# All 32 of layer 1's late modulation partial sums in layer 0's mixers, none in layer 1's projection

## What is computed

```
cond = jax.nn.silu(c)
for layer in range(DEPTH):
    mod = cond @ ada_w[layer] + ada_b[layer]
    sh1, sc1, g1, sh2, sc2, g2 = [m[:, None, :] for m in jnp.split(mod, 6, axis=-1)]
    h = rms_norm(x, norm_mix[layer]) * (1 + sc1) + sh1
    mix = mix_gla_gdn(h, ...) if layer % 2 == 0 else mix_swa(h, ...)
    x = x + g1 * mix
    h = rms_norm(x, norm_ffn[layer]) * (1 + sc2) + sh2
    x = x + g2 * moe(h, ...)
```

## Time and profile before

| | |
|---|---|
| median of 3 runs | 1645.1 us (1643.97 to 1645.26) |
| the profiled execution | 1644.02 us |
| its span | 1642.1 us |
| PE busy | 1373.0 us (84%) |
| DVE busy | 1102.9 us (67%) |
| ACT busy | 705.5 us (43%) |
| chain that ended last, by engine | PE 73%, DVE 13%, ACT 5%, DMA 5%, issue 3% |

### The profile page before, as it was taken

How to read it: one execution, slowest core, us unless ns; L and a number is a source line. 1 busy time by engine, 2 the same in 40 slices (tenths; PEclk the granted TensorE clock), 3 DMA queues, 4 the chain that set the end, 5 groups by cost and what they waited for, 6 DMA issues and landing times.

```text
span 1642.1 us, 15877 instructions
## 1 busy us (share of the span) xinstructions
PE 1373.0 (84%) x6192; PEld 1049.0 (64%) x6192; DVE 1102.9 (67%) x1258; ACT 705.5 (43%) x865; POOL 363.6 (22%) x135
## 2 busy tenths in 40 slices
PE   5899976759776987999999664976889689999992
PEld 1587765559664465888888542434764568888882
DVE  3757676567554464999899628675415659999994
ACT  1212333232123133777777521123642257777771
POOL 2100000000000000566664411000000015665641
PEclk9879987969888977999999876996979689999997
DMA  9678327120200354999999336253000659999964
GB/s 347 229 260 289 96 81 265 39 77 14 116 1 0 129 228 155 368 384 374 373 376 362 119 110 251 88 190 156 1 0 27 234 213 366 381 373 380 387 239 167
DMA packets 63440, 338.42 MB, mean 206 GB/s; under 512 B 11738, under 2 KB 11818, under 8 KB 49284
## 3 DMA queue, kind: packets, MB, share of 16 engines
q1 hardware_dynamic: 50868, 310.54, 50.8%
q0 software_dynamic: 11680, 23.43, 4.1%
q10 hardware_dynamic: 816, 3.43, 0.6%
HBM read 326.34 MB, written 28.84 MB: 216 GB/s over the span
## 4 chain that ended last, share of the span: by engine, by line
PE 73%; DVE 13%; ACT 5%; DMA 5%; issue 3%; POOL 1%; SPq 0%; DVEq 0%; ACTq 0%; POOLq 0%
PE ps L1333 12%; PE ps L1334 11%; PE ps L1335 11%; PE ps L1203 7%; PE ps L894 6%; PE ps L1225 5%; PE ps L901 2%; ACT work L1478 2%; PE ps L903 2%; PE ps L902 2%; DMA ring<-in_ada_w_dram 2%; DVE early_mod L2022 2%; PE ps L1251 1%; ACT work_r L1478 1%; PE ps L1280 1%
## 5 line engine op out<-in xcount | busy, mean ns | idle before, releaser
L801 POOL TENSOR_TENSOR work<-work,early_mod 128x1024 f32<-128x1024 f32 x33 | 175.7, 5324 | 181.0 <-ACT work L1478 181.0
L1335 PE MATMUL ps<-ring_r,work_r 128*128 128x512 f32 x536 | 214.4, 400 | 0.0
L1478 ACT ACTIVATE work<-ps 128x512 f32<-128x512 f32 (+4 forms) x142 | 90.8, 646 | 286.3 <-PE ps L1335 165.3
L894 PE MATMUL ps<-const,work 128*128 128x128 f32 x792 | 127.7, 306 | 98.9 <-DVE work L1994 29.9
L1333 PE MATMUL ps<-early_mod_r,work_r 128*128 128x512 f32 x468 | 189.4, 405 | 10.8 <-DVE work_r L2600 4.7
L2295 DVE TENSOR_TENSOR ring_r<-ring,early_mod_r 128x2048 fp32r<-128x2048 f32 x76 | 177.9, 2371 | 27.1 <-ACT early_mod_r L1478 26.6
L1334 PE MATMUL ps<-early_mod_r,work_r 128*128 128x512 f32 x468 | 186.6, 399 | 0.0
L894 PEld LDWEIGHTS ps<-const,work 128*128 128x128 f32 x792 | 107.4, 161 | 122.4 <-DVE work L1994 28.7
L1478 ACT ACTIVATE work_r<-ring 128x2048 fp32r<-128x2048 f32 (+2 forms) x87 | 133.2, 1555 | 56.3 <-PE ps L903 56.0
L1478 ACT ACTIVATE early_mod_r<-ring 128x2048 fp32r<-128x2048 f32 x79 | 147.5, 1908 | 0.0
L1333 PE MATMUL ps<-work_r 128*128 128x512 f32 x324 | 132.5, 409 | 7.3 <-DVE work_r L2600 4.9
(11 more groups left out here) (329 smaller groups left out, 2712.1 us busy)
## 6 DMA issues: line engine op xcount, KB each, us to landing
ring<-in_moe_w_up_dram SPq DMA_DIRECT2D x33, 2048.0 KB, 10.3
early_mod<-in_ada_w_dram SPq DMA_DIRECT2D x80, 512.0 KB, 4.5
ring<-in_moe_w_gate_dram SPq DMA_DIRECT2D x19, 2048.0 KB, 10.0
hT<-in_moe_w_down_dram SPq DMA_DIRECT2D x16, 2048.0 KB, 9.9
ring<-in_moe_w_down_dram SPq DMA_DIRECT2D x15, 2048.0 KB, 9.9
work<-in_moe_w_gate_dram SPq DMA_DIRECT2D x14, 2048.0 KB, 10.4
ring<-in_ab_w_in_dram SPq DMA_DIRECT2D x7, 2048.0 KB, 9.8
ring<-in_ada_w_dram SPq DMA_DIRECT2D x4, 2048.0 KB, 23.7
```

What stands on the lines that cost most here:

```text
L801: return nc.gpsimd.tensor_tensor(yb[buf], yb[buf], mod[:, 5 * D:6 * D], ALU.mult)
L894: return nc.tensor.transpose(dst, src, ident[0:k, 0:k])
L1335: return mm(out, a_hi, w_lo, start=False, stop=last_)
L1478: return nc.scalar.activation(out, in_, fn, **kw)
```

## The change

It moves the boundary `SIDE_B` from 8 to 10, so that units 64 to 79 join units 48 to 63 in the mixers, and `project_swa` holds none. The counts in the mixers become 8, 5, 2, 5 and 3 after each of four levels, 32 in all. The four blocks' sums lie in the four row tiles of `x`. With the blocks 8 and 9 gone from layer 1, SP issues no side load there, the wait for all puts ahead of L776 becomes a wait for the end of `project_swa` (`phase_done` 18), and so does POOL's wait ahead of L883. POOL's second clearing of `side_pad` is taken out.

```
-        SIDE_B = 8
+        SIDE_B = len(SIDE)
...
-            for c in ((1, 1, 1, 1, 1) if t + 1 < TT else (1, 0, 0, 0, 0)):
+            for c in (0, ) * 5:
...
             if SIDE_A <= i < SIDE_B:
-                return x.rearrange("p t d -> p (t d)")[:, 1024 * (i % 2):1024 * (i % 2) + 1024]
+                return x[:, i - SIDE_A]
...
-            for u in range(KD * SIDE_B, KD * len(SIDE)):
-                side_load(u)
-            side_put(len(SIDE) - 1)
             load_columns(("swo", 1), a["swa_w_out"][0], range(0, D, 512))
-            sp.wait_ge(side_out, 16 * len(SIDE))
+            sp.wait_ge(phase_done, 3 * 6)
             sp.dma_start(mod[:, 2048:6144], sum_rows[1][:, 2048:6144]).then_inc(sums_in[2], 16)
...
             pool.wait_ge(moe_done, 1)
-            nc.gpsimd.memset(side_pad, 0.0).then_inc(pad_ready, 1)
             norm_shift(1)
-            pool.wait_ge(side_out, 16 * len(SIDE))
+            pool.wait_ge(phase_done, 3 * 6)
             nc.gpsimd.dma_start(gain2, bc(a["norm_ffn"][1])).then_inc(gains_in[1], 16)
...
             def gla_gates():
-                mix_sides(5)
+                mix_sides(8)
                 dve.wait_ge(GATE_ACT.sem, GATE_ACT.at(0, "l"))
...
                 ins.then_inc(GATE_DVE.sem, GATE_DVE.one("zg"))
-                mix_sides(3)
+                mix_sides(5)
...
                         dve.wait_ge(GLA_DVE.sem, GLA_DVE.at(t, f"s{c}"))
-                mix_sides(1)
+                mix_sides(2)
                 dve.wait_ge(GLN_ACT.sem, GLN_ACT.at(0, "ss3"))
...
-                mix_sides(3)
+                mix_sides(5)
                 dve.wait_ge(PRE_ACT.sem, PRE_ACT.at(0, "expa"))
...
                     if l < 5:
-                        mix_sides(1)
+                        mix_sides(3)
```

## The result

| | before | changed |
|---|---|---|
| median | 1644.86 us, 4 runs (1643.97 to 1645.26) | 1662.6 us, 4 runs (1657.41 to 1665.14) |
| ratio | | 1.0104, interval 1.0082 to 1.0126 |
| profiled execution | 1644.02 us, span 1642.1 | 1663.34 us, span 1661.4 |
| granted TensorE clock, mean | 0.892 | 0.886 |

The change costs 17.7 us by the medians and 19.3 by the two profiled executions. The prediction was 1658.8 in a range of 1652 to 1665, so the median lies inside the range, near its upper end.

What follows compares the result with a forecast made beforehand. PE was taken to bound layer 1's projection, side sums and their loads the chain at the mixers' gates. Terms 5.8 + 1.1 + 1.4 + 4.1 + 1.9 = 14.3 us, nothing saved, gave 1658.3, median put at 1658.8, range 1652 to 1665.

Steps and rivals of the forecast that it cites:

- Taken out: Layer 1's projection: removing sixteen DVE units, 20.5 us, and their loads gains 0, at most 0.8 us, since PE bounds it.
- Moved later: Read-backs of both layers' sums, the reload of `x` and the `gain2` load start later but are covered: 0.
- Gates: Ahead of the gate, 5 units become 8; DVE time and loads start the gate 5.8 us later.
- Behind the gate: Between the gate and the next DVE step, 3 units become 5: 1.1 us late, bounds 0 and 3.3.
- Loop: Behind GLA's loop, 1 unit becomes 2; the variance waits for DVE: +1.4 us.
- `gdn_pre`: In `gdn_pre`, 3 units become 5, the last two waiting for loads: +4.1 us, bounds 3.8 and 6.8.
- Inverses: At four levels, 1 unit becomes 3; DVE needs 11.2 us against PE's 10.72: +1.9 us, bounds 1.0 and 3.0.
- The clock: PE's granted clock: level changes may fall a few matmul groups earlier or later; 0, bound 3 us either way.
- a stage beyond 533 us changes by more than 1 us: Sign that would show the forecast wrong: a stage later than 533 us whose length changes by over 1 us.
- The mixers absorb it: Rival: 57 us of idle DVE in the mixers takes the units, time stays 1644 to 1646; chance 0.07.
- The projection pays it back: Rival: units held up PSUM banks in layer 1's projection; removing 22.2 us of them gives 1636; chance 0.04.
- Loads bind harder: Rival: fourth units meet 7.5 us load landings and PE stays at low clock longer: about 1667; chance 0.12.

Runs made afterwards that it cites:

- the gates' half: Changed kernel with eight units left in layer 1's projection: 8, 5, 1, 3 in the mixer groups and 2, 2, 2, 1 a level; 1653.55 us, ratio 1.0048.
- the second trace: The changed kernel run again, unedited, beside the kernel before; 1657.54 us over 6 runs, ratio 1.0087.
- the levels' half: Changed kernel with eight units left in layer 1's projection: 5, 3, 1, 3 as before and 3 a level; 1650.81 us, ratio 1.0044.
- The delay: Kernel before with 15 clearings of `kz` added on DVE ahead of the gate, no side unit or load more; 1664.41 us, ratio 1.011.
- the one with 5, 4, 0 and 3: Kernel before with the output projection's weight chunks behind the side loads, sixteen mixer units at 5, 4, 0, 3 and one a level; 1643.77 us, ratio 0.9986.

## Why the prediction held, and where it did not

**Taken out: 0, and 0 measured.** The kernel without the sixteen units measured it directly, 0.9999.

**Moved later: 0.** SP's read-back was issued at 1134.75, 17.8 us after PE's last matmul of the projection at 1116.9, where "some 17 us later" was the estimate. The fold that needs it ran at 1230.02, 95 us on, and took its usual 3.49 us. The row of SP's queue:

```profile
1134.75 0.34 SPq L773 DMA_DIRECT2D early_mod<-sum_rows  x1
```

**Gates: 5.8 predicted, 6.4 and 6.8 measured**, 5.8 with one unit a level, and 5.2 in the gates' half. The mechanism is the predicted one, load by load; unit 51's load took 8.14 us instead of 7.78, and unit 55's 4.73 instead of 4.5. The pieces of the chain that are loads, here and in the two later groups:

```profile
271.74 8.14 DMA early_mod<-in_ada_w_dram
...
282.60 4.73 DMA early_mod<-in_ada_w_dram
...
294.79 5.45 DMA early_mod<-in_ada_w_dram
...
350.34 5.15 DMA early_mod<-in_ada_w_dram
```

**Behind the gate: 1.1, and 1.1** (1.3 in the second trace). **Loop: 1.4, and 1.4** from the first unit's start to the variance (2.59 us against 1.21), while the loop itself was 0.3 shorter. **`gdn_pre`: 4.1, and 4.1** (5.1 in the second trace, where the last load took 6.10 us instead of 5.15). **Inverses: 1.9, and 1.7**, with DVE's period of 11.2 us a level measured as 11.16. Together 14.3 predicted, 14.25 measured to `ku_b`, 16.3 in the second trace. That 14.3 met 14.25 so closely is in part luck: the gate cost 0.6 more, the loop and the inverses less, and the second trace is 2.0 away. What the terms are made of is shown: the gates' half gave the gates' two terms without the others, the levels' half that of the inverses alone, and the kernel with 8, 5, 2 and 5 but one unit a level the groups without the inverses, those of the loop and `gdn_pre` among them. These two were not tried one by one. The delay showed that lateness at the gate reaches the end.

Two sums of the prediction are off by little. It put the median 1.1 us above the profiled execution and yet arrived at 1658.8, where 1658.3 + 1.1 is 1659.4, and its inverses (423.2 against 421.2) give 2.0 and not 1.9.

**The clock: 0 with a bound of 3, and that is the mis-sized term.** I bounded it from one stretch of 5 us at the gates and looked for it only where PE idles longer. The granted clock differs elsewhere too, above all in the steps of the delta rule with their 480 small matmuls; there two executions of one kernel differ by 8.7 us, and all kernels together lie between 106.7 and 115.4. In the first trace of the changed kernel this stage was 3.6 us longer than before, in the second 5.1 shorter. Not all of that is accounted for: by the same working as above the kernel before spends 34 us of it at the low level (0.85 over 112), 3 less than the first trace and 13 more than the second, which would be 1.5 and 6.5 us at half speed. What the runs give is a bound, about 5 us either way in this stage, and not a cause. The steps took 111.8 us in the four kernels whose groups stand as before (5, 3, 1, 3, one a level), with or without a delay; 112.8 to 113.1 in the six traces of kernels with other groups and up to two a level; and 106.7, 106.7, 114.2 and 115.4 with three a level. The delay speaks against lateness as the cause, and units a level cannot be the only one. That three a level, where DVE falls behind PE, widens the spread is a reading of four traces; what sets the clock's pattern stays open. Of the 5.0 us by which the first trace's 19.3 exceed the forecast 14.3, the steps hold 3.6 and the last stage 2.3, less 1.3 in layer 1's projection and attention (on these two see below), and 0.6 lies ahead of the start.

**The sign "a stage beyond 533 us changes by more than 1 us" did appear**: -1.3 in layer 1's projection and attention, +2.3 in the last stage. In the other kernels, those without the sixteen units and the pure delay among them, the last stage took 422.1 to 423.1 us. So the 420.6 of the kernel before looks like a feature of its one profiled execution and not of the change; a second trace of that kernel was not taken. The sum was then made against an execution that was itself 1.5 to 2.5 us short there. The projection and attention took 207.6 to 207.7 us in three traces, the kernel before, the one without the sixteen units and the one with 5, 4, 0 and 3, and 206.4 to 206.7 in nine others; this 1 us lies in the attention and goes with no edit that I can name.

**The rivals.** "The mixers absorb it" falls by each row above, though it holds in part: two units a level cost nothing. "The projection pays it back" is refuted. "Loads bind harder" did not occur as put: the last load of each of these groups landed in 4.7 to 5.5 us in the first trace and 5.3 to 6.1 in the second, and the one ahead of it in 3.4 to 4.1, not 7.5. The upper group of runs, up to 1665, comes near its 1667 by the length of the steps instead.

The Trainium skill, page "DMA: Bandwidth & Descriptors", section "Anatomy of one DMA — SWDGE (gpsimd) path", gave an estimate of 3.2 us for 512 KB and so, in the prediction, a sum of about 11 (term by term I get 4.5 + 0 + 1.4 + 2.4 + 1.9, an estimate of about 10). The trace disagrees: the loads on the chain took 4.73 to 5.45 us, besides the one of 8.14 behind the weights, and the sum was 14.25. The Trainium skill, page "Perfetto Trace Analysis", section "Optimization Strategy", says that interleaving regimes may improve the time. Here moving the work cost time instead; what decided was which instruction stood behind each group, and not how long DVE idles in the stage.

## What to carry to other kernels

Idle time of an engine is not room. Work fits at a place only if the next instruction of that engine waits for something else for at least as long: the 0.72 us ahead of L2138 held no unit, the 2.17 us at each level held one, and 57 us of idle DVE in two stages took in about a third of the sixteen (14.25 us were paid of 22.2). Price each place by its own neighbour, and where units use a few staging buffers, count the units that were not loaded ahead from the issue of their loads (here the last of a group took 4.7 to 6.1 us to land), not by the instruction's 1.28 us: three more units ahead of the gate cost 6.4 us, two more in `gdn_pre` 4.1, about 2.1 each.

Before moving side work out of a stage, leave it out and time that: here one kernel showed that the giving side had nothing to give. The cover has an end, though: with 32 units in the projection the last ones ran behind its last matmul, and the pause of PE there grew by 6.6 us. And look at what the side loads queue behind; here, moving 4 MB of weights that nobody needed yet behind them was worth 2.3 us.

## What the hardware showed that I had not expected

- The same kernel, with the same 480 matmuls in a stage and the same instructions around them, took 106.68 and 115.35 us for that stage, at granted clocks of 0.90 and 0.84; the totals of ten runs fell into two groups some 6 us apart. One trace of this kernel tells a term that crosses such a stage no more closely than that.
- The length of that stage repeated to 0.03 us (111.75 to 111.78) in four kernels whose groups of units stand alike, though one of them reached it 18 us later than the others. Kernels with their units placed otherwise had 1 us more, or much less and much more. What links the order of the units to the level changes no run here shows.
- A 512 KB load behind 4 MB of weights on one queue took 7.78 and 8.14 us. With the weights behind it instead, the unit that waits for it ran at 275.12 and not at 278.95.
